# Four key pages of an attention slot transposed one at a time between the slot's other products

## The reference

```python
# prompt, one block of 128 queries
sc = jnp.einsum('bqhd,bkhd->bhqk', qb, k) * scale
sc = sc + cb.transpose(0, 2, 1)[..., None] - cum_k
sc = jnp.where(kpos[None, :] <= qpos[:, None], sc, -jnp.inf)
p = jax.nn.softmax(sc, axis=-1)
o = jnp.einsum('bhqk,bkhd->bqhd', p, v)

# sample: k_past = cache_k[page_table], v_past = cache_v[page_table]
s_past = jnp.einsum('bqhd,bkhd->bhqk', q, k_past) * scale
s_past = s_past + cn_t[..., :, None] + suf_t[..., None, :]
s_new = jnp.einsum('bqhd,bkhd->bhqk', q, k) * scale  # + decays, causal
p = softmax(concat([s_past, s_new]))
o = p[:p_len] @ v_past + p[p_len:] @ v
```

## Time and profile before

| what | before |
|---|---|
| time, median of 3 runs | 1812.11 us (1808.1 to 1812.4) |
| time of the profiled execution | 1809.96 us |
| its span, first to last instruction | 1807.8 us |
| TensorE busy, share of the span | 1580.4 us, 87% |
| VectorE, ScalarE, GpSimd | 48%, 31%, 14% |
| key transposes on TensorE (L976) | 1024 products, 140.8 us |
| key copies (L1163), VectorE | 128, 87.8 us, 686 ns each |
| key copies (L1163), ScalarE | 128, 74.9 us, 585 ns each |
| key and value loads | 512 of 256 KB |

### The profile page before, as it was taken

How to read it: one execution, slowest core, us unless ns; L and a number is a source line. 1 busy time by engine, 2 the same in 40 slices (tenths; PEclk the granted TensorE clock), 3 DMA queues, 4 the chain that set the end, 5 groups by cost and what they waited for, 6 DMA issues and landing times. The chain is left out here.

```text
span 1807.8 us, 32157 instructions
## 1 busy us (share of the span) xinstructions
PE 1580.4 (87%) x11702; PEld 1101.8 (61%) x11702; DVE 870.4 (48%) x1311; ACT 566.9 (31%) x965; POOL 244.2 (14%) x230
## 2 busy tenths in 40 slices
PE   5999998958999999998599998979952899999965
PEld 3444444647776767765399998944431567676731
DVE  2011111924565555555354645434344666766638
ACT  1000002102444444444234334300010556665622
POOL 0001010031001010000121313103231111111021
PEclk9999999978999999999699999989985999999987
DMA  8634443046999989996356464552113899999954
GB/s 331 236 119 166 156 154 94 18 160 229 362 326 322 335 296 334 310 306 208 102 134 186 124 183 124 139 199 70 47 50 143 316 378 419 419 418 418 404 186 183
DMA packets 226254, 411.60 MB, mean 228 GB/s; under 512 B 18844, under 2 KB 112221, under 8 KB 217942
## 3 DMA queue, kind: packets, MB, share of 16 engines
q1 hardware_dynamic: 208392, 345.44, 55.0%
q0 software_dynamic: 13152, 47.95, 7.4%
q10 hardware_dynamic: 4608, 16.78, 2.3%
HBM read 367.26 MB, written 42.85 MB: 227 GB/s over the span
## 5 line engine op out<-in xcount | busy, mean ns | idle before, releaser
L326 PE MATMUL ps<-w_w,h_hT 128*128 128x512 f32 x512 | 227.4, 603 | 7.5 <-issue 4.0
L1527 PE MATMUL ps<-mix_x_hi,mix_w_hi 128*128 128x352 f32 x576 | 188.5, 327 | 25.3 <-DVE mix_x_lo L1479 21.8
L2209 DVE TENSOR_TENSOR ex_w_lo<-we_w_gu,ex_w_hi 128x1024 fp32r<-128x1024 f32 x128 | 150.8, 1220 | 103.1 <-ACT ex_w_hi L2254 102.5
L1527 PE MATMUL ps<-mix_x_hi,mix_w_lo 128*128 128x352 f32 x576 | 187.2, 325 | 0.0
L1527 PE MATMUL ps<-mix_x_lo,mix_w_hi 128*128 128x352 f32 x576 | 186.5, 324 | 0.0
L326 PEld LDWEIGHTS ps<-w_w,h_hT 128*128 128x128 f32 x512 | 97.1, 192 | 126.7 <-issue 125.3
L2254 ACT CAST ex_w_hi<-we_w_gu 128x1024 fp32r<-128x1024 f32 x128 | 128.5, 1061 | 94.8 <-DMA we_w_gu<-w_exp_up 87.0
L976 PE MATMUL ps<-g_ident,at_k_pg 128*128 128x128 f32 x1024 | 140.8, 281 | 15.9 <-DVE at_kT L1163 15.8
L976 PEld LDWEIGHTS ps<-g_ident,at_k_pg 128*128 128x128 f32 x1024 | 115.5, 143 | 63.2 <-issue 38.6
L1569 DVE TENSOR_TENSOR mix_w_lo<-g_arena,mix_w_hi 128x1024 fp32r<-128x1024 f32 x73 | 125.7, 1753 | 41.0 <-ACT mix_w_hi L1554 28.1
L1163 ACT COPY at_kT<-ps 128x512 f32<-128x512 f32 x128 | 74.9, 585 | 179.1 <-PE ps L976 179.1
(11 more groups left out here) (386 smaller groups left out, 2337.0 us busy)
## 6 DMA issues: line engine op xcount, KB each, us to landing
at_k_pg<-cache_k SPq DMA_DIRECT2D x256, 256.0 KB, 4.1
at_v_pg<-cache_v SPq DMA_DIRECT2D x256, 256.0 KB, 4.2
we_w_gu<-w_exp_gate SPq DMA_DIRECT2D x32, 1024.0 KB, 8.9
we_w_gu<-w_exp_up SPq DMA_DIRECT2D x32, 1024.0 KB, 11.2
we_w_dn<-w_exp_down SPq DMA_DIRECT2D x32, 1024.0 KB, 8.1
g_arena<-w_in SPq DMA_DIRECT2D x49, 512.0 KB
h_extra<-w_ada SPq DMA_DIRECT2D x16, 1024.0 KB
y_rows<-ex_y ACTq DMA_DIRECT2D x32, 512.0 KB, 7.5
```

Source lines behind the costliest of these rows:

```text
L326: last = nc.tensor.matmul(ps[:, b, :], g.hT[:, k, t * P:(t + 1) * P], w[s][:, k, :], start=(k == 0), stop=(k == KD - 1))
L1527: last = nc.tensor.matmul(out, w[p][:, at], v[:, x, :], start=(i == 0 and k == 0), stop=(i == len(w_chunks) - 1 and k == 2))
L2209: nc.vector.tensor_tensor(w_lo[half][:, i], w_gu[s][:, i, half * KH:(half + 1) * KH, :], w_hi[half][:, i].bitcast(F32), ALU.subtract).then ...
```

## The change

The four pages of a slot, which were transposed in two pairs, are transposed one at a time. On TensorE page 0 stays at the slot's head, page 1 comes behind the prompt scores, page 2 behind the turn of the prompt weights (before the sample scores), and page 3 behind the sample values and the sample turn (before the prompt values). The q/k columns of the next head pair, which stood around the second pair of pages, now follow page 1 all together. VectorE copies page 2 behind its copies of q/k columns. ScalarE copies page 3 behind the exponential of the prompt unit, ahead of its copy of prompt values and the sample exponential. What is computed, the banks, the buffers and the counts of the semaphores stay the same.

```diff
--- before.py
+++ after.py
@@ -965,17 +965,16 @@
                                                 skip_group_check=True)
                     last.then_inc(c_pe, 1)
 
-                def key_columns(n, half):
-                    if n == 0:
+                def key_columns(n, j):
+                    if n == 0 and j == 0:
                         pe.wait_ge(qk_copied, 2)
-                    if half == 0:
+                    if j == 0:
                         pe.wait_ge(k_in[n % 4], 64 * (n // 4) + 64)
-                    for j in (2 * half, 2 * half + 1):
-                        pe.wait_ge(kT_copied[j % 2], 2 * n + half)
-                        for c in range(KC):
-                            last = nc.tensor.transpose(ps[:, 4 + j % 2, c * P:(c + 1) * P],
-                                                       k_pg[:, 4 * (n % 4) + j, c * P:(c + 1) * P], g.ident[:])
-                        last.then_inc(kT_full[j % 2], 1)
+                    pe.wait_ge(kT_copied[j % 2], 2 * n + j // 2)
+                    for c in range(KC):
+                        last = nc.tensor.transpose(ps[:, 4 + j % 2, c * P:(c + 1) * P],
+                                                   k_pg[:, 4 * (n % 4) + j, c * P:(c + 1) * P], g.ident[:])
+                    last.then_inc(kT_full[j % 2], 1)
 
                 def sample_scores(n):
                     u, pp = n // 4, n % 4
@@ -1122,14 +1121,16 @@
                         key_columns(n, 0)
                     if 0 <= n - DELAY < P_UNITS:
                         prompt_scores(n - DELAY)
+                    if n < S_STEPS:
+                        key_columns(n, 1)
                     for key in groups[:len(groups) // 2]:
                         qk_columns(*key)
-                    if n < S_STEPS:
-                        key_columns(n, 1)
                     for key in groups[len(groups) // 2:]:
                         qk_columns(*key)
                     if 0 <= n - DELAY - 1 < P_UNITS:
                         prompt_turn(n - DELAY - 1)
+                    if n < S_STEPS:
+                        key_columns(n, 2)
                     if 0 <= n - 1 < S_STEPS:
                         sample_scores(n - 1)
                     if n == DELAY - 2:
@@ -1138,6 +1139,8 @@
                         sample_values(n - V_LAG)
                     if n >= 5 and (n - 5) % 4 == 0 and (n - 5) // 4 < S_UNITS:
                         sample_turn((n - 5) // 4)
+                    if n < S_STEPS:
+                        key_columns(n, 3)
                     mm = n - DELAY - 3
                     if mm >= 0 and mm % 2 == 0 and mm // 2 < P_UNITS // 2:
                         prompt_values(mm // 2)
@@ -1323,10 +1326,10 @@
                         copy_qk(dve, nc.vector.tensor_copy, *key)
                     if 0 <= n - DELAY < P_UNITS:
                         prompt_max(n - DELAY)
+                    for key in groups[len(groups) // 2::2]:
+                        copy_qk(dve, nc.vector.tensor_copy, *key)
                     if n < S_STEPS:
                         copy_keys(dve, nc.vector.tensor_copy, 0, n, 1)
-                    for key in groups[len(groups) // 2::2]:
-                        copy_qk(dve, nc.vector.tensor_copy, *key)
                     if n == 0:
                         masks()
                     if n and n % 4 == 0 and n <= S_STEPS:
@@ -1394,14 +1397,14 @@
                         copy_keys(act, nc.scalar.copy, 1, n, 0)
                     for key in groups[1:len(groups) // 2:2]:
                         copy_qk(act, nc.scalar.copy, *key)
-                    if n < S_STEPS:
-                        copy_keys(act, nc.scalar.copy, 1, n, 1)
                     for key in groups[len(groups) // 2 + 1::2]:
                         copy_qk(act, nc.scalar.copy, *key)
                     if 0 <= n - DELAY - 1 < P_UNITS:
                         prompt_turn(n - DELAY - 1)
                     if 0 <= n - DELAY < P_UNITS:
                         prompt_exp(n - DELAY)
+                    if n < S_STEPS:
+                        copy_keys(act, nc.scalar.copy, 1, n, 1)
                     if n == DELAY - 2:
                         act.wait_ge(shifted, 1)
                         nc.scalar.activation(s_new[:], s_new[:], ACT.Exp).then_inc(c_act, 1)
```

## The result

| | before | changed |
|---|---|---|
| median (lowest to highest) of 5 runs each | 1810.84 us (1808.10 to 1812.40) | 1798.28 us (1792.88 to 1801.23) |
| ratio, 95% interval | | 0.9923, 0.9912 to 0.9935 |
| profiled execution, its span | 1809.96, 1807.8 | 1801.23, 1799.1 |
| TensorE busy in the page | 1580.4 | 1586.4 |

The ratio is 13.9 us of 1810.8 (11.8 to 15.9), the medians differ by 12.6, and the two profiled executions by 8.7. A second timing on another chip, with five runs of the changed kernel beside ten of before (an eleventh, of 2165 us at a granted clock of 0.73, is left out), gave 1799.62 us and 0.9938 (0.9922 to 0.9953), which is 11.2 us (8.5 to 14.1). The forecast was 9.2 us faster: its direction and its mechanism held, and its size was too small.

What follows compares the result with a forecast made beforehand. TensorE's stream bounds the attention stage, so only some 17 us of idle time can be won. 13.6 + 0.4 - 0.3 - 2.6 - 1.6 - 0.3 = 9.2 us faster, named 1802 us, range 1799 to 1806, chance 0.67.

Steps and rivals of the forecast that it cites:

- The first slots: Slot 3, eight q/k column groups in a row: 0 to 1 us lost, taken as 0.3.
- The waits of T2 in slots 2 modulo 4: Page 2's transposes waiting for VectorE's copy of page 0; moved behind the prompt weights' turn, all 13.6 us taken as gained.
- slot 6's loss: First head pair's slot 6, no prompt values ahead: page 1 waits for ScalarE's copy of page 3, 0.3 us lost.
- Waits put at nothing: Waits from VectorE's and ScalarE's new places, priced at zero; 3 us allowed in the forecast's range for first slots above.
- slots 3 modulo 4: T3 ahead of values, T1's wait for T2's: Page 3 ahead of prompt values loses 2.6 us (15 x 0.17); page 1's wait replacing page 2's gains 0.4 us.
- q/k columns, six slots: Next head pair's q/k column groups without pages between: third group finds its bank full; 6 x 0.27 = 1.6 us lost.
- The bound of 0.24: Part of slot 26's 1.42 us wait of page 2 that the move leaves uncovered; over four head pairs at most 1.0 us.
- (a): Rival: new VectorE and ScalarE places make waits in slots 26, q/k slots and slot 3; 3 us faster, 1809; chance 0.17.
- (b): Rival: splitting page pairs on TensorE costs 0.17 us per extra change of kind; 12 us slower, 1824; chance 0.06.
- (c): Rival: key and value loads, issued back to back, come late and pace the stage; 11 us slower, 1823; chance 0.05.
- (d): Rival: page 0's late copy delays maximum, page 2's copy and next page 0; 4 us slower, 1816; chance 0.05.
- the wide one: Range 1797 to 1812 us: the forecast with rival (a) and 2 us more on its fast side.

Runs made afterwards that it cites:

- t3_behind_t2: The changed kernel with page 3 transposed directly behind page 2 instead of at the slot's end; 1807.37 us, 0.9968 of the kernel before.
- t3_behind_values: The changed kernel with page 3 transposed behind the prompt values in all odd slots; 1799.10 us, 0.9932 of the kernel before.
- heads_later: The kernel before with VectorE's sample mask and sum one slot later, TensorE's order untouched; 1803.45 us (0.9965), timed again 1800.72 us (0.9946).

## Where the prediction went wrong, and what held

The mechanism held, VectorE's queue ahead of the copy of page 0, and so did the direction. What failed is the size: the sum of 9.2 us, and with it the time of 1802 us and the forecast's range of 1799 to 1806. The gain in the part of the stage to which the working speaks was 11.0 us in one course of the clock and 12.8 in the other. Three steps of the working were mis-sized, all in the same direction:

- The first slots, "0 to 1 us lost; I take **0.3**". The step looked at the bank of the column groups alone, and the window from which the working took the clock, 1.00, starts at 440 us, near their end, while the clock in the head was 0.84. Measured: nothing lost in one course of the clock, 1.7 us gained in the other.
- The waits of T2 in slots 2 modulo 4, 13.3 us with slot 6's loss. Measured: 14.1; 0.3 of the difference is slot 6, priced like slot 22, and the rest 0.05 in each of the others.
- Waits put at nothing: slot 4 (0.28 us) and those of T2 in slots 3 modulo 4 with two blocks of scores (0.15 each), because "the other 17" waits were taken to lie in two kinds of slot. With them the loss in slots 3 modulo 4 was 1.6 us in place of 2.2.

Term by term, from the slots' distances, at the same clock:

| term | forecast | measured |
|---|---|---|
| T2 behind the turn, slots 2 modulo 4, the first (slot 6) with its loss | +13.6 - 0.3 | +14.09 |
| slots 3 modulo 4: T3 ahead of values, T1's wait for T2's | -2.6 + 0.4 | -1.60 |
| q/k columns, six slots | -1.6 | -1.65 |
| slot 4 | 0 | +0.28 |
| head (slots 0 to 3), at a clock of 0.94 in both | -0.3 | 0.0 |
| sum | 9.2 | 11.1 |

(The measured terms add up to 11.1 and the second pair of traces to 11.0, as the distances of the other slots have up to 0.03 each in rounding and noise. In slot 63 and in the head, 0.43 us of a page is only counted on the other side of a slot's border; I took it out of both.)

*T2 in slots 2 modulo 4.* Right, and the largest term: 1.21 in slot 22, 1.46 in 26, 0.87 in 30, each 0.05 us more than the wait that I had read from starts and lengths. The bound of 0.24 that might remain in slot 26 did not remain: T2 starts without idle time. The reason was named in the prediction: with ScalarE's copy of T3 behind the exponential, VectorE's mask of sample output starts 5.48 us after slot 25's scores (577.99 to 583.47), before it was 5.92 (581.45 to 587.37), 0.44 earlier. It takes both new places of T3 to get that: t3_behind_t2 has ScalarE's and not TensorE's, and its mask starts at 5.90. In slot 6 the loss came (T1 waits 0.26 us for ScalarE), but I had priced its old wait like slot 22's, 1.16; by the same reading it was 456.18 - 454.58 - 0.21 = 1.39. So it still gained 1.14. The two rows of the kernel before:

```profile
447.52 1.06 PE L976 MATMUL ps<-g_ident,at_k_pg 128*128 128x128 f32 x8 [0.23 <-DVE at_kT L1163]
...
454.58 0.39 PE L1041 MATMUL ps<-at_qkT 66*128 66x128 f32 x2
...
456.18 1.09 PE L976 MATMUL ps<-g_ident,at_k_pg 128*128 128x128 f32 x8 [1.21 <-DVE at_kT L1163]
```

*Slots 3 modulo 4.* The 0.17 us in front of the prompt values came as said in each of 15 slots (+0.15 in slots 15, 31 and 47, and given back to that size by t3_behind_values). What was mis-sized is the gain against it. I had counted the old wait of T2 only where one block of scores leaves it bare. With two blocks, slots 11, 27, 43 and 59, it was 0.15 (as heads_later shows in slot 26), and it is gone as well: these slots rose by 0.03 and not by 0.21, one-block slots by 0.04. Slot 43 is an exception: +0.31 in both traces, with T1 waiting 0.54 us for ScalarE, whose copy of T3 began 1.03 us after that page (694.96 to 695.99) in place of 0.75:

```profile
694.96 0.86 PEld L975 LDWEIGHTS ps<-g_ident,at_k_pg 128*128 128x128 f32 x8 [0.84 <-issue]
...
695.99 0.59 ACT L1166 COPY at_kT<-ps 128x512 f32<-128x512 f32 x1 [2.23 <-PE ps L975]
```

ScalarE had nothing else to do for 2.23 us, so it isn't its queue. The same 0.28 us more stand in slot 22 of t3_behind_values (557.11 to 558.14). It falls on the same slot in every trace of the same order, and why is open.

*q/k columns.* To the hundredth: 0.28 in slots 18 and 0.42 in slots 19, of which 0.15 is the page ahead of the values, so 0.27 each. But the list of waits has 0.34 and 0.46 in products where I said 0.5 and 0.65; on the weight loads it is 0.61 and 0.72. It was the difference of the starts that was right, and what a row calls idle depends on which of the two one reads.

*Head and slot 4.* 0.3 us lost was a guess between 0 and 1. At a mean clock of 0.94 in both kernels nothing was lost. In the other course of the clock the head is 2.1 us shorter (29.29 against 31.40; 29.34 against 31.54 in t3_behind_values and heads_later say the same), of which 0.4 is the page that changed sides: 1.7 us gained. Slot 4 gained 0.28 that I had not looked for: the row at 447.52 above is T0 of slot 5, which waited 0.23 us for VectorE's copy of T2, since T2 stood right behind the scores. It was one of the 19 waits, in a third kind of slot.

*The rivals.* (a), half of it, needed a wait at T2 in slot 26 and 1 us in each column slot; the first didn't come, and the second stayed at 0.27. (b), splitting costs: slots 0 and 1 modulo 4 have the same pages split up, and in slots 8 to 61 their distances changed by at most 0.01 us, 28 times. A page between scores and turn, or between turn and sample scores, costs its weight loads and no more. The rule of the Trainium skill, TensorE: Matmul & The Clock Gate, "The mechanism" (Part 3), that weight loads overlap matmuls in flight only where the row group differs, is not borne out by this trace: all pages use 128 rows, and eight weight loads take 0.86 us beside a row of products of 1.09, in the changed kernel (589.47) as in the earlier trace rows. The prompt scores say it without the modelled ends: every product there has a weight load of its own over the same 66 rows, and they start 0.113, 0.220, 0.326 and 0.433 us apart for 128, 256, 384 and 512 columns. That is 0.107 us for each 128 columns and nothing for the load. (c), loads late: no wait, and most of a slot of cover to spare. (d), waits only move: behind the stage's first slots no product waits for VectorE's key copies any more, and the waits for ScalarE are those of T1 that were in the sum.

*The median.* 1798.3 lies below the forecast's own range of 1799 to 1806 and inside the wide one of 1797 to 1812, and the ratio's 13.9 us would put it at 1796.9, just outside both. The head's second course of the clock brings the sum to 12.8 us, which is within both intervals (11.8 to 15.9, and 8.5 to 14.1). Which of the untraced runs went which way isn't on record, and for what is left of the 13.9 no run shows a cause beyond the spread of the other stages.

## What to carry to other kernels

Where one engine is full, read the distance between the same instruction of neighbouring rounds, slot by slot: it shows a change of 0.05 us where the whole time can't show 3. Before you take the clock of a stage's middle for all of it, read it in the first slots too. Where a full engine waits for a copy, look first for what stands ahead of the copy in the copying engine's queue: moving that one thing gave as much here as reordering the full engine. And work out for each buffer the time of its round (from first write to its release) and put that much other work between its two users; a place with less, as page 3 behind page 2, gives the gain back elsewhere.

## What the runs showed of the hardware

The granted clock of TensorE behind an idle time of 2.1 us, in the same kernel at the same place, was 0.62 in one trace and 1.00 in another, with 2.4 us between the two heads. Thirteen traces show two courses: a head with a mean clock of 0.94 in seven of them, under either order, and in six a lower one, 0.84 with the order of before (two traces) and 0.88 with the new one (four). So kernels can't be compared by a stretch in which the clock changes unless it took the same course in both, but well by one with 1.00 throughout: the distances of 60 slots, 5 to 10 us long, agreed to 0.02 us on two chips.

A weight load of 64 or 32 columns starts 0.17 us late behind page transposes, and so does a page behind the 64-wide prompt values; behind the 32-wide sample values every one of them starts 0.84 us late. In eight traces with six orders of the work these two figures were the same each time; an order only sets how often they are paid.
